# A hybrid attention layer on one core: the sync queue waits for a weight chunk before it asks for x by rows, the tables and the next chunk

## What is computed

```python
u = rms_norm(h, attn_pre_g[l])
proj = u @ w_in[l]                 # 1024 x 1952
c_q, c_kv, k_r = proj[..., :256], proj[..., 256:384], proj[..., 384:416]
moba_qkv = proj[..., 416:]         # q, k and v of 8 heads of 64
mla_o = mla_attention(c_q, c_kv, k_r, ...)            # latent attention, 8 heads
moba_o = moba_attention(rope(q), rope(k), v)          # block-sparse attention, 8 heads
h = h + rms_norm(concat(mla_o, moba_o) @ w_out[l], attn_post_g[l])
u = rms_norm(h, mlp_pre_g[l])
h = h + rms_norm(square(relu(u @ w_up[l])) @ w_down[l], mlp_post_g[l])
```

## Time and profile before

| | |
|---|---|
| median of three runs | 562.42 us (562.3 to 562.56) |
| the profiled execution: its time | 562.25 us |
| its span, first to last instruction | 560.5 us |
| PE busy | 548.9 us, 98% of the span |
| DVE, ACT, POOL busy | 392.2, 293.4, 92.2 us |
| DMA | 99.66 MB, mean 178 GB/s over the span |
| granted TensorE clock, mean | 0.998 |

### The profile page before, as it was taken

The page is one execution under the profiler, slowest core; times in us unless marked ns, Lnnn a source line. Parts: engine busy times, 40 slices in busy tenths (PEclk is TensorE's granted clock), DMA queues, the critical chain, the costliest instruction groups (busy, mean ns, idle before and its releaser), DMA issues.

```text
span 560.5 us, 7840 instructions
## 1 busy us (share of the span) xinstructions
PE 548.9 (98%) x2730; PEld 451.9 (81%) x2730; DVE 392.2 (70%) x745; ACT 293.4 (52%) x612; POOL 92.2 (16%) x152
## 2 busy tenths in 40 slices
PE   9999999999999999999999999999999999999994
PEld 8888898876656888988888888888888888888883
DVE  5359473487785366367766775779777989778897
ACT  6563172688884364463344335344465656656561
POOL 1263110355784012200000000000000001000003
PEclk9999999999999999999999999999999999999999
DMA  8933652000002940387778886787975565605403
GB/s 289 370 123 104 201 165 76 0 2 2 0 2 76 340 149 1 108 297 272 229 277 279 278 283 229 276 279 265 357 280 195 181 216 167 219 21 204 150 1 150
DMA packets 43454, 99.66 MB, mean 178 GB/s; under 512 B 3232, under 2 KB 20896, under 8 KB 40096
## 3 DMA queue, kind: packets, MB, share of 16 engines
q1 hardware_dynamic: 42992, 98.54, 51.0%
q10 hardware_dynamic: 432, 0.74, 0.4%
HBM read 81.44 MB, written 15.73 MB: 173 GB/s over the span
## 4 chain that ended last, share of the span: by engine, by line
PE 91%; DMA 3%; DVE 2%; POOL 2%; ACT 1%; issue 1%; ACTq 0%; DVEq 0%; POOLq 0%
PE bank L1327 28%; PE bank L1328 27%; PE bank L1329 27%; PE bank L1539 3%; PE bank L1558 3%; POOL probs L527 1%; DMA w_raw<-in_w_in 1%; DMA x_raw<-in_x_cols 1%; PE bank L1504 1%; DVE w_lo L883 1%; PE bank L1333 1%; DVE bank L1000 1%; ACT w_hi L575 1%; ACT probs L665 0%; PE bank L1463 0%
## 5 line engine op out<-in xcount | busy, mean ns | idle before, releaser
L1327 PE MATMUL bank<-uT_hi,w_hi 128*128 128x512 f32 (+1 forms) x344 | 129.3, 376 | 0.8 <-DVE w_lo L883 0.8
L1328 PE MATMUL bank<-uT_lo,w_hi 128*128 128x512 f32 (+1 forms) x344 | 128.8, 374 | 0.0
L1329 PE MATMUL bank<-uT_hi,w_lo 128*128 128x512 f32 (+1 forms) x344 | 128.7, 374 | 0.0
L1327 PE MATMUL bank<-w_hi,a_hi 128*128 128x512 f32 x224 | 87.2, 389 | 0.0
L1329 PE MATMUL bank<-w_hi,a_lo 128*128 128x512 f32 x224 | 87.2, 389 | 0.0
L1328 PE MATMUL bank<-w_lo,a_hi 128*128 128x512 f32 x224 | 87.1, 389 | 0.0
L883 DVE SCALAR_TENSOR_TENSOR w_lo<-w_raw,g_up,w_hi 128x256 fp32r<-128x256 f32 x128 | 52.1, 480 | 48.4 <-ACT w_hi L575 48.4
L575 ACT ACTIVATE w_hi<-w_raw,g_up 128x256 fp32r<-128x256 f32 x128 | 53.0, 496 | 45.6 <-PE bank L1329 24.8
L1327 PEld LDWEIGHTS bank<-uT_hi,w_hi 128*128 128x128 f32 x344 | 64.7, 188 | 12.9 <-issue 1.1
L1328 PEld LDWEIGHTS bank<-uT_lo,w_hi 128*128 128x128 f32 x344 | 64.8, 188 | 11.5
L1329 PEld LDWEIGHTS bank<-uT_hi,w_lo 128*128 128x128 f32 x344 | 64.7, 188 | 11.4
(11 more groups left out here) (161 smaller groups left out, 871.3 us busy)
## 6 DMA issues: line engine op xcount, KB each, us to landing
stage<-in_w_down SPq DMA_DIRECT2D x17, 1024.0 KB, 4.9
w_raw<-in_w_up SPq DMA_DIRECT2D x16, 1024.0 KB, 8.4
pair_sums<-stage SPq DMA_DIRECT2D x13, 1024.0 KB, 9.9
w_raw<-in_w_down SPq DMA_DIRECT2D x10, 1024.0 KB, 6.7
w_raw<-pair_sums SPq DMA_DIRECT2D x10, 1024.0 KB, 4.8
w_raw<-in_w_in SPq DMA_DIRECT2D x6, 1024.0 KB, 7.5
w_raw<-in_w_out SPq DMA_DIRECT2D x4, 1024.0 KB, 4.8
stage<-pair_sums SPq DMA_DIRECT2D x3, 1024.0 KB, 4.8
```

Source lines behind the costliest of these rows:

```text
L1327: nc.tensor.matmul(out, lh, rh, start=start, stop=False)
L1328: nc.tensor.matmul(out, lh, rl, start=False, stop=False)
L1329: return nc.tensor.matmul(out, ll, rh, start=False, stop=stop)
```

## The change

SP now waits, behind `in_chunk(2)`, until `raw_in[0]` has reached 32, which is when the rows of group 0's fourth block and chunk 2 have landed. Everything that SP asks for later stands behind this wait. No instruction of another engine is touched, and none is moved.

```diff
@@ -370,6 +370,7 @@
                     first_x(k + 1)
             sp.dma_start(g_in[:, :], attn_pre_g).then_inc(g_in_in, 16)
             in_chunk(2)
+            sp.wait_ge(raw_in[0], 32)
             for t in range(NT):
                 sp.dma_start(x_sb[:, t, :], x_v[t]).then_inc(x_in[t], 16)
             sp.dma_start(rope_sb[:, :, :], rope_table.rearrange("(t p) c -> p t c", p=P)).then_inc(tab_in, 16)
```

## The result

| | before | changed |
|---|---|---|
| median | 562.41 us (6 runs, 561.75 to 562.59) | 565.69 us (6 runs, 563.89 to 567.32) |
| ratio | | 1.0061 (0.6% slower), 95% interval 1.0041 to 1.0081 |
| profiled execution: time, span | 562.25, 560.5 us | 563.89, 562.1 us |
| mean granted clock of the runs | 0.998 (profiled) | 0.996, 0.994, 0.993, 0.996, 0.993, 0.993 |

The change is slower, as forecast, but by 3.3 us in the median and not by 1.7. The profiled execution is the fastest of the six. So the table says where to look: not at this trace alone, but at what the other five executions do beyond it.

A forecast was written before the change was run, and what follows sets the result against it. PE, busy 98%, was taken as the bound. No gain at group 1 and 1.7 us lost ahead of group 2 made 562.25 + 1.7 = 563.95 us profiled, 564.1 as median, range 562.8 to 565.6.

The forecast's parts named there:

- the chain: From chunk 3's landing through the latents' factors and rotations to PE's group 2; claimed to have no slack.
- PE's stop of 1.95 us (0.25 + 1.7) shouldn't cost it its clock.: Ahead of group 2: PE stands still 1.95 us, and its granted clock was expected to stay up.
- the sum: Whole kernel: PE's gain at group 1 worth nothing, its stop ahead of group 2 costs 1.7 us; 563.95 us profiled.
- Chunk 3 lands later by 2.0 us: Chunk 3's landing, which starts ACT on it: moved from 27.6 to 29.6 us, with a 2.0 us start-up.
- the same bytes start from empty engines: DMA between chunk 2's and chunk 3's landings: same x, tables and chunk 3 bytes, plus a start-up of 2.0 us.
- So the chain moves by 1.25 to 2.0 us; I take 1.7.: Latents' factors and rotations ahead of group 2: delayed 1.7 us, less than chunk 3's 2.0.
- worth nothing: PE's gain at group 1, 0.1 us expected, at most 0.8: lost again by waiting longer ahead of group 2.
- I take 0.1 us.: Chunk 2's landing: 0.1 us sooner with x held back, within bounds of 0 and 2.4 us.
- chunk 2 at 17 or before: Chunk 2's landing time: a landing this early was named as a sign that the forecast is wrong.
- rival A: Chunk 2 lands up to 2.4 us sooner with x held back; no slower, 562.0 to 562.4 us; chance 0.18.
- The covers: Spare time in group 1: some 2 us for x's factors, 0.9 us for chunk 3's lo part in the second half.
- rival B: Full start-up, chunk 3 after 30.5 us; PE also stops ahead of group 1's second half; 565.2 us, chance 0.12.

The follow-up runs named there:

- a1: The changed kernel run again with no edit, for a second profile; 566.79 us, ratio 1.0081.
- a2: The changed kernel with 36 small matmuls of zeros ahead of PE's wait for the rotations before group 2; 565.26 us, ratio 1.0045.
- a3: The kernel before, transfers untouched, with PE waiting ahead of group 2 for all four rotations in place of two; 567.3 us, ratio 1.0088.
- b3: The kernel before, transfers untouched, with PE waiting ahead of group 2 for three rotations in place of two; 564.3 us, ratio 1.0039.
- b1: The changed kernel with chunk 3 asked for ahead of the rotary table and the gains; 563.0 us, ratio 1.0016.
- b2: The changed kernel with SP's wait for chunk 2 moved behind the four x requests, ahead of the tables; 562.03 us, ratio 0.9989.

## Why the prediction was wrong

The direction and the chain were right. The step that failed is this one: *"PE's stop of 1.95 us (0.25 + 1.7) shouldn't cost it its clock."* In 10 of the 12 runs of the changed kernel the mean clock is 0.994 or less, and a1's trace shows the fall to 1.2 GHz, at a price of about 1.6 us; a2, which fills the stop, is 1.5 us under a1 in the median and has no low mean clock. My evidence was one row of the kernel's end, and it breaks off too early. The same trace two us later reads

```profile
558.00:559.00 1.00, 0.00 (x0) 0.00 (x0) 0.01 (x1) 0.00 (x0) 0.00 (x0) 0.55 0.79 305
```

There the clock fell 5.0 us after the end of PE's last matmul, but that is one case: at the ends of the ten traces it fell 2.3 to 5.2 us after it, and in a1 2.3 us into the stop. A stop of 2.61 us stands both in the trace of the change, without a fall, and in that of a1, with one. What decides between the two is open.

The other steps, of which two were put too small as well:

- *The sizes of the miss.* In the mean of its six runs the change costs 3.4 us (565.75 against 562.34). Four of the six have a mean clock of 0.994 or less, so at 1.6 us each the clock makes up about 1.0 us of this, and the later start of group 2 about 2.4, where the sum has 0 and 1.7. These are estimates, since only one of the six has a trace. In a2, without the clock's share, the change costs 2.9 us in the median.
- *Chunk 3 lands later by 2.0 us.* On average the wait puts it 2.9 us further behind chunk 2. The start-up itself was sized well; the premise that failed is that "the same bytes start from empty engines". In the trace of before 2.65 MB move between chunk 2's request and its landing, in that of the change 1.96 MB: in the first, engines that are through with their part of chunk 2 go on with x, in the second they stand idle. Between the landings of chunk 2 and chunk 3 some 3.5 MB move without the wait (before, a3, b3) at 370 GB/s, and 3.8 MB with it (change, a1, a2). By an estimate from these numbers the larger amount is 0.7 us of the 2.9 and the start-up 2.2.
- *"So the chain moves by 1.25 to 2.0 us; I take 1.7."* The chain doesn't shrink: the second rotation keeps its 20.8 to 21.2 us behind ACT's start on chunk 3.
- *The stop itself.* Predicted 1.95 us, measured 2.61 in both traces. In the trace of the change PE reached the place 0.7 us sooner than before, which I had counted as "worth nothing"; for the start of group 2 that is right, but it makes the stop longer. In a1 PE was only 0.2 us sooner, and the rotation 0.5 us later than in the first trace.
- *The match of the profiled execution* (563.89 against 563.95) is luck. Chunk 2 landed at 16.79 and not at 18.65, and chunk 3 came 12.6 us behind it and not 10.95. The two misses cancel, and the chain starts at 29.46 where 29.6 was expected.
- *"I take 0.1 us."* No gain shows in the mean of the landings (7.5 and 7.3 us). The first trace, 16.79, meets the sign that I had named as wrong ("chunk 2 at 17 or before"), and nearly all bytes of chunk 2 do arrive as early as rival A has it. A's price, no slower, was not seen: even with chunk 2 at 16.79 the kernel lost 1.6 us.
- *The covers.* That of x's factors held in the traces. That of group 1's second half was just used up in the change and a1, where a weight load waited 0.5 us but PE hardly did, and broke in a2 with chunk 3 near 31.4: rival B's mechanism, in a single execution.
- *"562.25 + 1.7 ... 0.17 under the median."* The sum was made against an execution of before with a wait of 0.25 us ahead of group 2. In a3 and b3 it would have been about 1 us. That hid that the place was already a stop.

## What to carry to other kernels

Here the queue served chunk 2 in 7.5 us with x behind it and in 7.3 without, so a wait to protect the transfer at its head bought nothing. Its price was the start-up, and the part of x that the engines would have carried before chunk 2's last packets were in. If a chunk is late, move what stands ahead of it and isn't needed yet (here 288 KB of tables, about 2 us) behind it. And a stop of the matrix engine has two prices, its length and the clock; the second comes in some executions and not in others, so one trace can't exclude it.

## What the runs showed of the hardware

- The granted clock fell to 1.2 GHz near the end of a stop of PE in a1, 2.3 us into it, and in a3 0.3 us after PE had gone on. It was low from 50.6 to 54.1 us in the first and from 51.8 to 55.2 in the second, nearly all of it full work.
- How often the mean clocks show a fall goes with the length of the stop, of which each kernel has one or two traced: all five runs of a3 (4.09 us), 10 of 12 of the changed kernel (2.61), three of eight of b3 (2.41), two of twelve of b1 (1.87), none of eleven of b2 (1.51). 36 small matmuls of zeros in the stop, and none of a2's six runs shows one.
- Transfers of 1024 KB asked for at the same place took 6.4 to 8.1 us from request to use in ten traces. In a2 nearly all of it had moved 2.1 us before it landed.
- From empty, the DMA engines took between one and two us to come to flow: x is asked for at 16.80, and 33 GB/s flow in 17 to 18 us and 238 in 18 to 19.
- 288 KB of tables in small rows, asked for ahead of chunk 3, put it 1.8 to 2.1 us further behind chunk 2. Their bytes at 384 GB/s are 0.8 us.
